# Gated-delta stage of a two-block model: head pairs prepared one pair further ahead, beta moved into the decay exponent, the end decay moved from the keys to the values

## The reference, cut to what matters

```python
def gdn_scan(q, k, v, g, beta, s0):
    gcum = jnp.cumsum(g, axis=-1)
    decay = jnp.exp(jnp.where(incl, gcum[..., :, None] - gcum[..., None, :], -jnp.inf))
    k_beta = k * beta[..., None]
    a_strict = jnp.where(strict, jnp.einsum('bhcik,bhcjk->bhcij', k_beta, k) * decay, 0.0)
    rhs = jnp.concatenate([v * beta[..., None], k_beta * jnp.exp(gcum)[..., None]], axis=-1)
    sol = lax.linalg.triangular_solve(a_strict, rhs, left_side=True, lower=True, unit_diagonal=True)
    u, w = sol[..., :V], sol[..., V:]
    attn = jnp.einsum('bhcik,bhcjk->bhcij', q, k) * decay
    q_dec = q * jnp.exp(gcum)[..., None]
    k_end = k * jnp.exp(gcum[..., -1:] - gcum)[..., None]
    def step(S, inp):
        v_new = ui - jnp.einsum('bhqk,bhkv->bhqv', wi, S)
        o = jnp.einsum('bhqk,bhkv->bhqv', qd, S) + jnp.einsum('bhqs,bhsv->bhqv', ai, v_new)
        S = S * dec[..., None, None] + jnp.einsum('bhsk,bhsv->bhkv', ke, v_new)
        return S, o
```

## Time and profile before

| | us |
|---|---|
| median of 3 runs | 3763.33 (3760.58 to 3765.33) |
| profiled execution: span | 3761.4; no other time of it is given |
| this stage | 972 to 1367.5, PE of the next one from 1372.1 |
| first level-5 product of the four pairs | 1074.97, 1152.16, 1229.38, 1313.81 |
| start of their recurrences | 1099.83, 1178.03, 1253.37, 1332.2 |

### The profile page before, as it was taken

How to read it: one execution, slowest core, us unless ns; L and a number is a source line. 1 busy time by engine, 2 the same in 40 slices (tenths; PEclk the granted TensorE clock), 3 DMA queues, 4 the chain that set the end, 5 groups by cost and what they waited for, 6 DMA issues and landing times. The chain is left out here.

```text
span 3761.4 us, 50123 instructions
## 1 busy us (share of the span) xinstructions
PE 3581.7 (95%) x20018; PEld 2980.0 (79%) x20018; DVE 1968.9 (52%) x3065; ACT 1505.8 (40%) x2515; POOL 470.1 (12%) x362
## 2 busy tenths in 40 slices
PE   6999999899887789999999999999999999999998
PEld 4688888787676778888888788888888888888886
DVE  7455554467556634755455553536533444454543
ACT  3222222255555443555565642324322444452332
POOL 1000000144211000010011160120000000025021
PEclk8999999999999999999999999999999999999998
DMA  9744323322533445422223163335634646543332
GB/s 361 260 134 134 117 95 101 101 89 63 182 113 91 109 137 174 127 83 87 85 79 90 48 208 97 95 87 111 126 117 122 127 92 108 113 130 101 95 94 87
DMA packets 580504, 448.38 MB, mean 119 GB/s; under 512 B 64454, under 2 KB 500114, under 8 KB 579504
## 3 DMA queue, kind: packets, MB, share of 16 engines
q1 hardware_dynamic: 572080, 421.18, 40.4%
q10 hardware_dynamic: 6048, 19.14, 1.3%
q0 software_dynamic: 2144, 4.87, 0.4%
HBM read 387.61 MB, written 57.46 MB: 118 GB/s over the span
## 5 line engine op out<-in xcount | busy, mean ns | idle before, releaser
L2192 DVE TENSOR_TENSOR w_lo<-w,w_hi 128x512 fp32r<-128x512 f32 x429 | 291.3, 698 | 502.4 <-ACT w_hi L2185 501.9
L2185 ACT ACTIVATE w_hi<-w 128x512 fp32r<-128x512 f32 x429 | 260.7, 625 | 479.8 <-PE od_acc L2171 147.7
L4324 DVE TENSOR_TENSOR w_lo<-w,w_hi 128x512 fp32r<-128x512 f32 x260 | 232.7, 901 | 353.0 <-ACT w_hi L4217 351.7
L4183 PE MATMUL ta_acc<-u_hi,w_hi 128*128 128x512 f32 x960 | 375.1, 391 | 2.7 <-POOL u_lo L4118 1.4
L4185 PE MATMUL ta_acc<-u_hi,w_lo 128*128 128x512 f32 x960 | 373.7, 389 | 0.0
L4184 PE MATMUL ta_acc<-u_lo,w_hi 128*128 128x512 f32 x960 | 373.5, 389 | 0.0
L4217 ACT ACTIVATE w_hi<-w 128x512 fp32r<-128x512 f32 x260 | 163.5, 630 | 440.5 <-PE ta_acc L4185 433.3
L2169 PE MATMUL od_acc<-u_hi,w_hi 128*128 128x512 f32 x768 | 304.7, 397 | 0.0
L2171 PE MATMUL od_acc<-u_hi,w_lo 128*128 128x512 f32 x768 | 299.3, 390 | 0.0
L2170 PE MATMUL od_acc<-u_lo,w_hi 128*128 128x512 f32 x768 | 299.0, 389 | 0.0
L2169 PE MATMUL ev_acc<-u_hi,w_hi 128*128 128x512 f32 x608 | 250.8, 412 | 12.2 <-DVE w_lo L2192 4.1
(11 more groups left out here) (747 smaller groups left out, 8116.1 us busy)
## 6 DMA issues: line engine op xcount, KB each, us to landing
w<-in_o_w_in_dram SPq DMA_DIRECT2D x260, 256.0 KB, 7.5
w<-in_e_w_in_dram SPq DMA_DIRECT2D x144, 256.0 KB, 3.0
p_w<-in_w_in_dram SPq DMA_DIRECT2D x70, 512.0 KB, 6.2
mod_w<-in_w_ada_dram SPq DMA_DIRECT2D x32, 1024.0 KB, 11.9
w<-in_ple_gate_w_dram SPq DMA_DIRECT2D x128, 256.0 KB, 2.8
gate_w<-in_w_ada_dram SPq DMA_DIRECT2D x16, 1024.0 KB, 5.8
z_w<-in_w_in_dram SPq DMA_DIRECT2D x64, 256.0 KB, 3.0
w<-in_e_w_out_dram SPq DMA_DIRECT2D x64, 256.0 KB, 2.7
```

The source lines that it names most:

```text
L2185: act.activation(self.w_hi[m % self.ring][:], self.w[m % self.ring][:], ACT.Copy).then_inc(self.hi_set, 1)
L2192: eng.tensor_tensor(self.w_lo[m % self.ring][:], self.w[m % self.ring][:], self.w_hi[m % self.ring][:].bitcast(F32), ALU.subtract).then_in ...
L4183: pe.matmul(bank, hi, hi_x[:, k, :], start=(k == 0), stop=False)
L4324: dve.tensor_tensor(self.w_lo[m % RING][:], self.w[m % RING][:], self.w_hi[m % RING][:].bitcast(F32), ALU.subtract).then_inc(self.lo_set, 1)
```

## The change

The change keeps all stages and data layouts and rewrites the order in `gdn_stage`, with these new pieces:

1. ACT takes ln(beta) once, and DVE puts it into the exponent's bias (`ncum`), so the decay matrices carry beta. `decayed` becomes two products of 1024 and 512 elements for a head. `v_new` is then an unscaled copy, made in the four latent chunk steps only; `v_end`, the value times beta and the end decay, replaces `k_end`, and PE uses the token-order keys as they are.
2. The norms are taken apart: of q in the level phase of pair j for pair j+2, of k at its end and in chunk steps 0 and 1, with products and decays of pair j+2 in the recurrence of pair j. Buffers grow for that: `attn` from 4 to 6, `q_n` from 2 to 4.
3. The triangle of pair j+1: 14 steps in the level phase of pair j (`TRI_EARLY`), then one or two at each slot of the chunk steps; it is turned in chunk step 4.
4. `finish(j)` moves into the level phase of pair j+1, and so does its store.
5. POOL does the query products of a pair first, then the mask sums, both earlier than before.
6. SP: the blocks that need no turn are written out ahead of the others, x waits for its own two writes, `gather` of head 2j+4 stands between write and read, that of the next head behind the read.
7. Filler goes, except three groups. Tail steps: 8 behind pair 2, 12 in the level phase of pair 3, 8 in its recurrence, 4 at the end; before, 20 stood behind pair 2.

```diff
                 sp.wait_ge(tri_step, TRI_STEPS * (j + 1))
+                solved(1, 1, tri)
+                solved(0, 0, tri)
                 sp.wait_ge(tri_turned, j + 1)
-                for n in range(2):
-                    for d in range(2):
-                        src = tri if n == d else blk
-                        sp.dma_start(blocks_out[j % 2, n, d].rearrange("h c b i j -> (h c b) (i j)"),
-                                     src[tri_rows(d)].rearrange("p i j -> p (i j)")).then_inc(tri_out, 16)
+                solved(1, 0, blk)
+                solved(0, 1, blk)
...
+            for hd in range(2, 4):
+                load_q(hd)
+                load_arg(hd)
             sp.dma_start(y_lo[:].bitcast(F32), y_ready.rearrange("b p t -> p b t")).then_inc(y_loaded, 16)
...
                     scatter_out(j + 1)
-                    if not ahead:
-                        tail.load_weights(sp, 6)
+                if ahead:
+                    gather(a)
+                if more:
                     scatter_in(j + 1)
...
-                            if d == 0 and j < PAIRS - 1:
-                                stay_busy(pe, bank[5], ones, 3)
                             pe.wait_ge(s_set, S_STEPS * j + 2 * n - 1 + d)
...
-                            out = bank[d][:, hh * P:(hh + 1) * P]
-                            last = pe.matmul(out, y_m[j % 2][:, hh, c, d, :], v_tok[(2 * j + hh) % 4][:, c, :], start=True, stop=(n == 0))
-                            if n > 0:
-                                last = pe.matmul(out, w_neg[:, hh, c, d, :], state[:, (n - 1) % 2, hh, d, :], start=False, stop=True)
+                            for hh in range(2):
+                                last = pe.matmul(bank[d][:, hh * P:(hh + 1) * P], w_neg[:, hh, c, d, :], state[:, (n - 1) % 2, hh, d, :],
+                                                 start=False, stop=(hh == 1))
                         last.then_inc(v_ready, 1)
...
+                            pe.wait_ge(v_end_set, S_STEPS * j + 2 * n + d + 1)
                             for hh in range(2):
-                                last = pe.matmul(bank[2 + d][:, hh * P:(hh + 1) * P], k_end[:, hh, c, d, :], v_new[:, hh, d, :],
+                                last = pe.matmul(bank[2 + d][:, hh * P:(hh + 1) * P], k_tok[(2 * j + hh) % 4][:, c, :], v_end[:, hh, d, :],
                                                  start=True, stop=True)
                             last.then_inc(s_ready, 1)
...
-                    pe.wait_ge(s_set, S_STEPS * j)
-                    stay_busy(pe, bank[3], ones, 23)
                 level5_t(j)
                 if more:
-                    turn_v(a)
+                    turn_k(a)
...
-                if more:
-                    products(a)
+                if j > 0:
+                    finish(j - 1)
...
-                if more:
-                    products(b)
+                if ahead:
+                    k_sums(a + 2)
+                    k_sums(b + 2)
                 steps(j)
-                if j + 2 < PAIRS:
-                    norms(j + 2, lambda: finish(j))
-                    continue
-                if j == PAIRS - 2:
-                    pe.wait_ge(attn_set, GDN_H)
+                if more and not ahead:
+                    pe.wait_ge(v_copied, 2 * GDN_H)
                     pe.wait_ge(k_copied, 2 * GDN_H)
                     tail.pe_steps(pe, 2 * TAIL)
-                if j == PAIRS - 1:
-                    tail.pe_steps(pe, TAIL)
-                finish(j)
-                if j == PAIRS - 2:
-                    tail.pe_steps(pe, 3 * TAIL)
+            finish(PAIRS - 1)
...
-                            ins = act.activation(v_new[:, hh, d, :], bank[d][:, hh * P:(hh + 1) * P], ACT.Copy,
-                                                 scale=tabs[:, 0, c, d, hd:hd + 1])
-                        ins.then_inc(v_set, 1)
+                        if n < CHUNKS - 1:
+                            for hh in range(2):
+                                hd = 2 * j + hh
+                                ins = act.activation(v_end[:, hh, d, :], bank[d][:, hh * P:(hh + 1) * P], ACT.Copy,
+                                                     scale=tabs[:, 2, c, d, hd:hd + 1])
+                            ins.then_inc(v_end_set, 1)
+                    if n >= CTX_CHUNKS:
+                        for d in range(2):
+                            act.activation(v_new[:, :, d, :], bank[d][:, 0:256].rearrange("p (h q) -> p h q", h=2), ACT.Copy
+                                           ).then_inc(v_new_set, 1)
...
+                    if j + 1 < PAIRS and n == 4:
+                        turn_tri(j + 1)
...
+                if j > 0:
+                    norm_exp(j - 1)
...
+                if ahead:
+                    inverse_q(a + 2)
+                    inverse_q(b + 2)
                 if more:
                     queries(a)
                     queries(b)
+                if ahead:
+                    square_k(a + 2)
+                    square_k(b + 2)
                 steps(j)
...
             for j in range(PAIRS):
                 if j + 1 < PAIRS:
                     identity(j + 1)
+                    queries(2 * j + 2)
+                    queries(2 * j + 3)
                 if j + 2 < PAIRS:
                     argument(2 * j + 4)
                     argument(2 * j + 5)
-                if j + 1 < PAIRS:
-                    queries(2 * j + 2)
-                    queries(2 * j + 3)
...
-            dve.tensor_scalar(ncum[:], tabs[:, 4], -1.0, None, ALU.mult).then_inc(ncum_set, 1)
+            dve.tensor_scalar(ncum[:], tabs[:, 0], 1.0e-38, None, ALU.max).then_inc(ncum_set, 1)
             dve.memset(x_by_d[:], 0.0).then_inc(cleared, 1)
...
+            dve.wait_ge(beta_ln, 1)
+            dve.tensor_tensor(ncum[:], ncum[:], tabs[:, 4], ALU.subtract).then_inc(ncum_set, 1)
+            dve.tensor_tensor(tabs[:, 2], tabs[:, 2], tabs[:, 0], ALU.mult).then_inc(ncum_set, 1)
...
-                for c in range(CHUNKS):
-                    if c in (0, 4):
-                        dve.wait_ge(kk_ready, 2 * hd + 1 + c // 4)
-                    for d in range(2):
-                        ins = dve.scalar_tensor_tensor(a_t[hd % 4][:, c, d, :], bank[6 + c // 4][:, (c % 4) * P:(c % 4 + 1) * P],
-                                                       tabs[:, 0, c, d, hd:hd + 1], a_t[hd % 4][:, c, d, :], ALU.mult, ALU.mult)
-                    if c in (3, 5):
-                        ins.then_inc(a_set, 1)
+                dve.wait_ge(kk_ready, 2 * hd + half + 1)
+                lo, n = 4 * half, 4 - 2 * half
+                dve.tensor_tensor(a_t[hd % 4][:, lo:lo + n], bank[product_banks(hd)[1 + half]][:, 0:n * P].rearrange("p (c q) -> p c q", c=n)
+                                  .unsqueeze(2).to_broadcast([P, n, 2, P]), a_t[hd % 4][:, lo:lo + n], ALU.mult).then_inc(a_set, 1)
...
+                at = TRI_EARLY
                 for n in range(CHUNKS):
                     for d in range(2):
                         c = ORDER[d][n]
-                        between(n)
-                        if n < CHUNKS - 1:
-                            dve.wait_ge(s_ready, S_STEPS * j + 2 * n + d + 1)
...
-                        between(n)
+                        for slot in range(2):
+                            for _ in range(1 if n < 2 else 2):
+                                if more and at < TRI_STEPS:
+                                    triangle(j + 1, at)
+                                    at += 1
...
+                                if n == 2 and d == 1:
+                                    attention(a)
+                                if n == 3:
+                                    decayed(a, d)
+                                if n == 4 and d == 0:
+                                    turned(a)
+                                if n == 4 and d == 1:
...
+                for n in range(6 if more else 0):
+                    triangle(j + 1, n)
+                if j > 0:
+                    finish(j - 1)
...
+                for n in range(6, TRI_EARLY if more else 0):
+                    triangle(j + 1, n)
+                if ahead:
+                    norm_q(2 * j + 4)
+                    norm_q(2 * j + 5)
+                steps(j)
```

680 lines of the change are left out of this document (413 added, 267 removed).

## The result

The kernel after takes **3774.62 us**, the median of six runs (3771.24 to 3779.0); six runs of the kernel before beside them give 3764.01 (3760.58 to 3766.64). The ratio is 1.003, with an interval of 1.0021 to 1.0040: slower by 10.6 us. The prediction was 3763, no change.

A forecast was written before the change was run, and what follows sets the result against it. PE is busy 95% of the span, mostly on untouched projection; the triangle's turn, set by DVE's chain, was to pace the pairs. Terms -3.5 - 2.2 + 6.5 - 12.5 + 12.7 - 1 sum to 0.0, giving 3763 us, range 3752 to 3775.

The forecast's parts named there:

- Level phase, ACT: Pair 0's level phase: 5.1 us of added ACT work on 24.8, so the recurrence starts at 29.9.
- Pair 1: Second head pair: finish waits for ACT's exponent, triangle steps and q norms wait out GpSimd; 83.7 us, +6.5.
- The pair clock as the measure: Time from a pair's first level-5 product; the change is worth how much earlier the triangle's turn can start.
- GpSimd waited out: DVE's triangle operations, t = 26 to 38, wait out every GpSimd operation; bounds 0 and 11.6 us per pair.
- The rival of small waits: Triangle operations slip in beside GpSimd, so first states come at 32 and 33; -19, 3744 us; chance 0.34.
- Recurrence and hand-over: In pair 0 the turn starts at 63.7, 28.6 us after the first state; 11.3 more to the next pair.
- Pair 2: Third head pair prepares nothing further and keeps 8 of 20 projection steps; 71.9 us against 84.4, -12.5.
- Pair 3 and the end: Last head pair takes over projection steps, 54.5 us against 41.8, +12.7; then the way from o to its store, -1.
- Start and mix: Before pair 0: y comes 7 to 8 us later, mix loses waits; -3.5, bounds -9.4 and +4.
- The clock falls with the filler: Without filler, PE in pairs 0 to 2 may run at 0.8 for 0.95; +16, 3779 us; chance 0.22.
- The change does not do what it says: Turn still after the recurrence, state updates queued behind triangle steps; +5.1 in pairs 0 and 1, about 3774 us; chance 0.08.

The follow-up runs named there:

- early q loads: Kernel after with a pair's two q loads issued ahead of the second head's gather instead of behind the triangle block's load: 3763.23 us, 0.9998 of the kernel before.
- filler put back: Kernel after with filler products added at five places where PE idles in pairs 0 and 1: 3778.5 us, 1.0040 of the kernel before.
- arithmetic, no filler: Kernel before with beta in the exponent and end decay on values, no chunk-step or hand-over filler, decay-table product ahead of the logarithm wait: 3758.41 us, 0.9985.

## Why the prediction was wrong

The step that failed is *Level phase, ACT*: "So the recurrence starts at 24.8 + 5.1 = 29.9 in pair 0." It counted ACT's added operations and not what the first of them waits for. The text had the fact: under *Pair 1* it says that SP loads the data of q's squares only behind the triangle block, "landing 8.2, so ACT's level 5 ends at 11.4", and it used it for `finish` alone. Two things were wrong with that. The landing is at t = 12.5, not 8.2: the issue comes at 6.7 and the data 5.8 later. And the evacuation behind the squares is what PE's next level needs. The block for the triangle was late in the same way, at t = 12.1 (1085.54) for the predicted 8.3. Measured starts of the recurrence: 37.1 and 39.5 against 29.9 and, for pair 1 with its 2.3 of work for o, 32.2. With the loads moved: 29.7 and 32.8, the numbers of the prediction. The missed term is 16.0 us of the stage in the profiles, 11.4 by the medians. What remains is close to the predicted 0: the stage is 3.9 us shorter than before in its profile, the fastest of ten, and the median, 3763.23, is the one that was predicted.

Point by point:

- *The pair clock as the measure*: right. The pairs' sum explains the 12.1 us of the stage and the 10.6 of the median.
- *GpSimd waited out*: right. In pair 1 four triangle operations take 2.4 to 3.5 us, one for each GpSimd operation. In pair 0 only one does (1113.05, 3.57 us), since DVE stood idle while GpSimd worked; with early q loads it is three there (2.57, 2.45 and 3.53). Its size: 9.5 us for the stage. The rival of small waits priced them at 19; that rival is excluded by the rows and was too dear as well.
- *Recurrence and hand-over*: predicted 45.1 in pair 0 (63.7 + 11.3 - 29.9) and 51.5 in pair 1, measured 46.3 and 50.7. That they agree is in part luck, since the way there was another. The prediction let DVE's chain set the turn, at t = 63.7. DVE had solved the triangle at 59.5 in spite of the late level phase, and the turn came at 71.6: for 12 us it stood behind other work in ACT's order. Moved one step up it comes 4.3 us sooner, and the median is the same, so this place costs little. Behind the turn the product came after 11.8 us (predicted 11.3).
- *Pair 2*: -13.9 for -12.5. *Pair 3 and the end*: +8.6 for +11.7. *Start and mix*: -1.8 for -3.5; y came later, as said (first mix product 1014.72 for 1013.5).
- *The clock falls with the filler*: its first half is right (0.98 to 0.80), its price of 16 us is not seen. That a slower PE is hidden while DVE, ACT and DMAs set the pace, as the prediction held against it, would explain this, but is argued and not shown. Clock and filler together moved the total by no more than about 4 us either way.
- *The change does not do what it says*: its 3774 is the measured time, by another mechanism. That rival had the turn after the recurrence and the hand-over unchanged; the turn comes inside the recurrence, and PE's filler and wait at the hand-over fell from 8.2 us to 3.3. The right number is no sign of the right cause.

Two things stay open. The four other executions with filler put back lie at 3778.3 to 3779.9 and the profiled one at 3773.21; why is not known, and so the sign of the clock's few us is not settled. And pair 1 is held at 80 to 84 us once q is early. The largest part found is GpSimd's, 8 us (83.8 against 75.7), and the profile of the early q loads shows where it ends up, in PE's wait for the first state:

```profile
1192.62 1.22 PE L572 MATMUL gdn_bank<-gdn_state,gdn_w_neg 128*128 128x128 f32 x4 [7.03 <-DVE gdn_state L1093]
```

What holds the rest of it was not taken apart.

## What to carry to other kernels

When a step moves ahead of something urgent on an in-order engine, ask first when its *input* lands, and follow that load back through the issuing queue: here a pair of loads behind another head's gather and a wait cost 11 to 16 us. An operation that nobody needs yet should not stand ahead of an evacuation that the next product needs. Deeper pipelining removed the visible gap here and paid for it with waits inside the longer queues. Price the pieces that need no new order by themselves, since here these alone (arithmetic, no filler) beat the whole change.

## What the runs showed of the hardware

- In these traces a DVE operation with two SBUF inputs that meets a GpSimd one lasts until that one ends, however small it is: 3.48 us for 96 elements a partition, begun 0.9 us into a mask sum of 3.8, in the row above. In a row of short ones, each GpSimd operation catches one of them: 2.45, 2.44, 3.54, 3.52.
- The granted clock of a stage full of short dependent steps fell by a fifth (0.98 to 0.80) with the new order and without filler. Sums of k took 4.4 us for 2.7, and no run shows a change of the total beyond 4 us that goes with the clock.
- The stage's first product starts between 972.1 and 975.7 us in the kernels' profiled executions, with the same code ahead of it. The total of one execution therefore carries up to 3.6 us that is not the stage's. Pair clocks inside a profile are free of that, but each is one execution too.
